# First modulation of a decoder step in two column halves, over the first two tiles of the input projection

## The reference, cut to what matters

```python
def _front(x, c, g_mix, w_ada, b_ada, w_in):
    mod = (jax.nn.silu(c) @ w_ada + b_ada)[:, None, :]
    shift1, scale1, gate1, shift2, scale2, gate2 = jnp.split(mod, 6, axis=-1)
    h = _rmsnorm(x, g_mix) * (1 + scale1) + shift1
    ...
    q, k, v, b_gate, c_gate, u_in, gate_a, gate_b = jnp.split(h @ w_in, pts, axis=-1)
```

## Time and profile before

| | |
|---|---|
| median of 3 runs | 789.85 us (789.43 to 791.33) |
| profiled execution | 789.53 us, span 787.8 us |
| PE busy | 694.5 us, 88% of the span |
| first matmul of tile 0 / of tile 1 | 41.97 us / 50.78 us |
| last `w_ada` of the first modulation landed | 33.37 us |

### The profile page before, as it was taken

The page is one execution under the profiler, slowest core; times in us unless marked ns, Lnnn a source line. Parts: engine busy times, 40 slices in busy tenths (PEclk is TensorE's granted clock), DMA queues, the critical chain, the costliest instruction groups (busy, mean ns, idle before and its releaser), DMA issues.

```text
span 787.8 us, 12170 instructions
## 1 busy us (share of the span) xinstructions
PE 694.5 (88%) x5003; PEld 532.7 (68%) x5003; DVE 318.0 (40%) x701; ACT 165.7 (21%) x323; POOL 123.9 (16%) x189
## 2 busy tenths in 40 slices
PE   2589999999999999999999999779999988788820
PEld 1289989879899889999997455555565554455500
DVE  2162232135688773322234765425232322211235
ACT  4062222221154442112110111111111111100001
POOL 2400000410006001000000100123333332222112
PEclk9989999999999999999999999769999999988975
DMA  9843546856143438421105972779999999999873
GB/s 293 331 160 140 215 174 267 324 215 222 54 133 118 151 105 331 169 69 67 55 27 177 415 294 87 255 291 400 415 414 413 411 413 417 416 414 416 356 302 151
DMA packets 40399, 198.48 MB, mean 252 GB/s; under 512 B 8174, under 2 KB 8358, under 8 KB 24720
## 3 DMA queue, kind: packets, MB, share of 16 engines
q1 hardware_dynamic: 31088, 175.42, 57.3%
q0 software_dynamic: 8352, 21.81, 8.0%
q10 hardware_dynamic: 904, 0.47, 0.3%
HBM read 188.54 MB, written 17.40 MB: 261 GB/s over the span
## 4 chain that ended last, share of the span: by engine, by line
PE 81%; DMA 6%; DVE 4%; issue 4%; ACT 2%; SPq 1%; POOL 1%; POOLq 0%; DVEq 0%
PE bank L1632 31%; PE bank L1878 16%; PE bank L1833 7%; PE bank L1900 7%; DMA arena<-in_w_in 5%; PE bank L1776 4%; PE bank L1871 2%; PE bank L1773 2%; PE bank L1570 2%; PE bank L1668 2%; PE bank L1731 1%; PE bank L1794 1%; PE bank L1895 1%; DMA arena<-y_scratch 1%; PE bank L1714 1%
## 5 line engine op out<-in xcount | busy, mean ns | idle before, releaser
L1632 PE MATMUL bank<-h_parts,w_parts 128*128 128x260 f32 x2160 | 273.4, 286 | 0.8 <-DVE w_parts L1068 0.6
L1632 PEld LDWEIGHTS bank<-h_parts,w_parts 128*128 128x128 f32 x2160 | 263.8, 189 | 9.9 <-issue 8.2
L1878 PE MATMUL bank<-arena,arena_b 128*64 128x256 f32 x704 | 89.8, 412 | 13.5 <-issue 9.1
L1068 DVE TENSOR_TENSOR w_parts<-arena,w_parts 128x1024 fp32r<-128x1024 f32 x46 | 56.2, 1222 | 71.3 <-ACT w_parts L897 71.1
L1878 PEld LDWEIGHTS bank<-arena,arena_b 128*64 128x64 f32 x704 | 57.6, 148 | 39.5 <-issue 12.3
L1422 DVE TENSOR_TENSOR arena_b<-bank,arena_b 128x128 f32<-128x128 f32 x32 | 9.3, 292 | 129.8 <-ACT arena_b L1000 129.7
L897 ACT ACTIVATE w_parts<-arena 128x1024 fp32r<-128x1024 f32 x46 | 48.4, 1052 | 55.9 <-DMA arena<-in_w_in 41.9
L829 POOL DMA_INDIRECT y_scratch<-arena_b x32 | 33.2, 1037 | 161.9 <-DVE arena_b L1447 154.4
L1833 PE MATMUL bank<-arena,arena_b 128*128 128x512 f32 x128 | 56.7, 597 | 0.0
L1878 PE MATMUL bank<-arena_b 128*64 128x256 f32 x320 | 40.1, 407 | 6.1 <-issue 5.3
L1900 PE MATMUL bank<-arena,arena_b 128*64 128x512 f32 x176 | 42.3, 593 | 0.8 <-DVE arena_b L1428 0.8
(11 more groups left out here) (301 smaller groups left out, 761.1 us busy)
## 6 DMA issues: line engine op xcount, KB each, us to landing
arena<-in_w_gate_up SPq DMA_DIRECT2D x44, 1024.0 KB, 29.1
arena<-in_w_in SPq DMA_DIRECT2D x46, 512.0 KB, 4.9
arena<-in_w_ada SPq DMA_DIRECT2D x22, 1024.0 KB, 7.2
arena<-in_w_down SPq DMA_DIRECT2D x20, 1024.0 KB
arena_b<-in_w_gate_up SPq DMA_DIRECT2D x20, 1024.0 KB
arena_b<-in_w_down SPq DMA_DIRECT2D x20, 512.0 KB
arena_b<-in_x_prompt SPq DMA_DIRECT2D x8, 512.0 KB, 7.8
arena_b<-q_scratch POOLq DMA_DIRECT2D x3, 1024.0 KB, 5.7
```

The lines of the kernel that those rows point to most:

```text
L1068: dve.tensor_tensor(w_parts[:, n % 2, 1], ring[:, n % WRING], w_parts[:, n % 2, 0], ALU.subtract).then_inc(s_wlo, 1)
L1632: ins = pe.matmul(ps[s][:, 0:HALF], w_parts[:, n % 2, wp, k], h_parts[:, hp, k, s * HALF:(s + 1) * HALF], start=(k == 0 and hp == 1), stop ...
L1878: ins = pe.matmul(ps[2 + b][R * hh:R * hh + R, 0:2 * P], hTe[:, b, c * P + jj * R:c * P + jj * R + R], w_gu[slot][jj][:, c, :, hh * P:(hh ...
```

## The change

The first modulation is computed in two halves of the features. Half j gives shift1 and scale1 for the 512 features of chunks 4j to 4j + 3. Its weights are laid out ahead in DRAM as `w_ada0`, four DMAs of 1 MB for each half, and each is one `first_step(half, s)`: two chunks by shift and scale, 4 matmuls into four quarters of 32 partitions of one bank, in which even and odd chunks have quarters of their own; a matmul with `both_quarters` (`turn_mods`) turns and adds them. SP issues x, half 0, tiles 0 and 1, half 1. PE does half 0, the chunks 0 to 3 of tile 0, the chunks 0 to 3 of tile 1 (other banks), and then the chunks 4 to 7 of both in turn; the four steps of half 1 stand between those of the chunks 0 to 3. ACT and DVE do `split(1)` within the h of chunks 0 to 3. The bias comes in two lots: ACT issues four DMAs of 9 rows of one piece of 2 KB at the old place, and four of two pieces before chunk 4. DVE's first memset is 2048 columns instead of 1536, and one small addition makes `both_quarters`. Some semaphores are merged. The diff, cut to this:

```diff
-TURNED = (2, 4, 5, 7)
+TURNED = (2, 4, 5, 7, 2, 4, 5, 2)
...
+        ada0 = [[region("SPLIT", (4 + 2 * s) * D, 2 * D) for s in range(4)],
+                [region(("CACHE", "QK")[s // 2], 2 * (s % 2) * D, 2 * D) for s in range(4)]]
+        ada0 = [[r.rearrange("p (k j n) -> p k j n", k=2, j=2) for r in half] for half in ada0]
+        ada = cube(region("CACHE", 0, 4 * D), 2)
...
+        tile_bank = [(ps[3], ps[7]) if n == 1 else (ps[0], ps[1]) for n in range(len(ORDER))]
+        row_bank = [(ps[2 + 2 * (n % 2)], ps[3 + 2 * (n % 2)] if n else ps[6]) for n in range(NQKV)]
+
+        def h_done(k):
+            return k + 2 if k < 4 else k + 3
...
-                if a >= 4:
-                    sp.wait_ge(s_adamm, a)
-                dst = ada0[a] if a < 4 else ada
+                sp.wait_ge(s_adamm, a + 4)
                 for k in range(2):
-                    sp.dma_start(dst[:, k], ada_v[a // 4, a % 4, k]).then_inc(signal, 16)
+                    sp.dma_start(ada[:, k], ada_v[a // 4 - 1, a % 4, k]).then_inc(s_ada[3], 16)
+
+            def load_first(half):
+                for s in range(4):
+                    sp.dma_start(ada0[half][s].rearrange("p k j n -> p (k j n)"), w_ada0[half, s]
+                                 ).then_inc(s_adb[s // 3] if half else s_ada[s], 16)
 
             def load_tile(n):
                 sp.dma_start(ring[:, n % WRING].rearrange("p k n -> p (k n)"), w_in[n]).then_inc(s_win[n % WRING], 16)
 
-            for a in range(4):
-                load_ada(a)
-                if a == 0:
-                    for i in range(5):
-                        sp.dma_start(x[0:rows[i], i], xp_v[i] if i < 4 else xs_v).then_inc(s_x[i], 16)
-            load_tile(0)
-            for n in range(1, len(ORDER)):
+            for i in range(5):
+                sp.dma_start(x[0:rows[i], i], xp_v[i] if i < 4 else xs_v).then_inc(s_x[i], 16)
+            load_first(0)
+            for n in range(WRING):
+                load_tile(n)
+            load_first(1)
+            for n in range(WRING, len(ORDER)):
...
+                sp.wait_ge(s_wlo, n - WRING + 1)
...
+                at = 12 * (j % 2)
+                act.dma_start(ada_bias[32 * j:32 * j + 1 + TS, at:at + 4].rearrange("p s n -> p (s n)"),
+                              b_v[0, j:j + 1].to_broadcast([1 + TS, 512])).then_inc(s_bada, 16)
+                j, cc = k // 4, k % 4
+                if k == 2:
+                    split(1)
+                if k == 4:
+                    for jj in range(4):
+                        act.dma_start(ada_bias[32 * jj:32 * jj + 1 + TS, 4:12].rearrange("p (g s) n -> p g (s n)", g=2),
+                                      b_v[1:3].rearrange("g j n -> j g n")[jj:jj + 1].to_broadcast([1 + TS, 2, 512])
+                                      ).then_inc(s_bada, 16)
+                if cc == 0:
+                    act.wait_ge(s_mod, j + 1)
                 act.wait_ge(s_xT, k + 2)
-                j, cc = k // 4, k % 4
-                at_least(act, s_hD, k - 1)
+                if k >= 3:
+                    act.wait_ge(s_hD, h_done(k - 3))
...
+            def first_out(j):
+
+                if j == 0:
+                    dve.wait_ge(s_bada, 64)
+                dve.wait_ge(s_adamm, 4 * j + 4)
+                dve.tensor_tensor(mods[:, 0:4], cube(ps[6][:], 4), ada_bias[:, 12 * j:12 * j + 4], ALU.add
+                                  ).then_inc(s_adaev, 1)
+                dve.wait_ge(s_modT, j + 1)
+                src = cube((ps[0], ps[6])[j][:, 0:256], 4)
+                shift, scale = 32 * j, 64 + 32 * j
+                dve.tensor_copy(modT[:, :, shift:shift + 1 + TS], src[:, :, 0:1 + TS])
+                link(dve.scalar_tensor_tensor(out=modT[:, :, scale:scale + 1 + TS], in0=src[:, :, 32:33 + TS],
+                                              scalar=1.0, in1=gmixT[:, 4 * j:4 * j + 4].unsqueeze(2)
+                                              .to_broadcast([P, 4, 1 + TS]), op0=ALU.add, op1=ALU.mult))
+                dve.engine_nop().then_inc(s_mod, 1)
+                if j == 0:
+                    split(0)
+
...
+                for k in range(4 * j, 4 * j + 4):
+                    dve.wait_ge(s_hA, k + 1)
+                    if k % 2:
+                        link(dve.tensor_copy(h_parts[:, 0, k, 0:TP], h_tmp[:, k % 3]))
+                    dve.tensor_tensor(h_parts[:, 1, k, 0:TP], h_tmp[:, k % 3], h_parts[:, 0, k, 0:TP], ALU.subtract
+                                      ).then_inc(s_hD, 1)
+                    if k == 2:
+                        split(1)
...
-            for n in range(NQKV):
+            for n in range(1, NQKV):
                 split(n + 1)
-                if n:
-                    by_rows(n - 1)
+                by_rows(n - 1)
...
+            def first_step(half, s):
+
+                if half == 0:
+                    pe.wait_ge(s_ada[s], 16)
+                else:
+                    pe.wait_ge(s_adb[s // 3], 16 if s == 3 else 48)
+                if half and s == 0:
+                    pe.wait_ge(s_adaev, 1)
+                for kk in range(2):
+                    for jj in range(2):
+                        q = 32 * (2 * jj + kk)
+                        ins = pe.matmul(ps[6][q:q + 32, :], cvec[:, 2 * s + kk], ada0[half][s][:, kk, jj],
+                                        start=(s == 0), stop=(s == 3), skip_group_check=True)
+                ins.then_inc(s_adamm, 1)
+
+            def turn_mods(half):
+
+                pe.wait_ge(s_adaev, half + 1)
+                for cc in range(4):
+                    ins = pe.matmul((ps[0], ps[6])[half][:, 64 * cc:64 * cc + 64], mods[:, cc], both_quarters,
+                                    start=True, stop=True, skip_group_check=True)
+                ins.then_inc(s_modT, 1)
+
             def turn_x(k):
-                at_least(pe, s_hA, k - 3)
+                at_least(pe, s_hA, 5 if k == 7 else k - 3)
                 for i in range(NB):
-                    ins = pe.transpose(ps[TURNED[k % 4]][:, i * P:(i + 1) * P], x[:, i, k * P:(k + 1) * P], idn)
+                    ins = pe.transpose(ps[TURNED[k]][:, i * P:(i + 1) * P], x[:, i, k * P:(k + 1) * P], idn)
                 ins.then_inc(s_xT, 1)
 
-            for a in range(2):
-                ada_step(a)
+            def tile_step(n, k):
+
+                if k == 0:
+                    pe.wait_ge(s_whi, n + 1)
+                    pe.wait_ge(s_wlo, n + 1)
+                pe.wait_ge(s_hA, k + 1)
+                pe.wait_ge(s_hD, h_done(k))
+                for s in range(2):
+                    for wp, hp in ((0, 1), (0, 0), (1, 0)):
+                        ins = pe.matmul(tile_bank[n][s][:, 0:HALF], w_parts[:, n, wp, k],
+                                        h_parts[:, hp, k, s * HALF:(s + 1) * HALF],
+                                        start=(k == 0 and hp == 1), stop=(k == KD - 1 and wp == 1),
+                                        skip_group_check=True)
+                    if k == KD - 1:
+                        ins.then_inc(s_half, 1)
+
+            for s in range(4):
+                first_step(0, s)
             pe.wait_ge(s_xn, 5)
             for k in range(KD):
                 ins = pe.transpose(ps[3][:, k * TS:(k + 1) * TS], x[0:TS, 4, k * P:(k + 1) * P], idn[0:TS, 0:TS])
             ins.then_inc(s_xT, 1)
+            turn_x(0)
+            turn_mods(0)
+            for k in range(1, 4):
+                turn_x(k)
+            first_step(1, 0)
+            for k in range(4):
+                if k == 2:
+                    first_step(1, 1)
+                tile_step(0, k)
+                if k < 3:
+                    turn_x(4 + k)
+            first_step(1, 2)
             for k in range(3):
-                turn_x(k)
-            for a in range(2, 4):
-                ada_step(a)
-            turn_x(3)
-            pe.wait_ge(s_adaev, 1)
-            for cc in range(4):
-                ins = pe.transpose(ps[0][:, cc * P:(cc + 1) * P], mods[:, cc], idn)
-            ins.then_inc(s_modT, 1)
+                tile_step(1, k)
+            first_step(1, 3)
+            tile_step(1, 3)
+            turn_mods(1)
+            for k in range(4, KD):
+                if k == 5:
+                    turn_x(7)
+                for n in range(2):
+                    tile_step(n, k)
```

More of the change, by code:

```diff
@@ L1989, in laid_out @@
         out[name] = cached(t[name], s)
-    out |= {name: t[name] for name in ("cache_conv", "c_prompt", "c_sample", "g_mix", "w_ada", "b_ada")}
+    out |= {name: t[name] for name in ("cache_conv", "c_prompt", "c_sample", "g_mix")}
+    first = t["w_ada"][0][:, 0:2 * D].reshape(4, 2, P, 2, 2, 512)
+    out["w_ada0"] = first.transpose(4, 0, 2, 1, 3, 5).reshape(2, 4, P, 2 * D)
+    out["w_ada"] = t["w_ada"][:, :, 2 * D:]
+    out["b_ada"] = t["b_ada"]
     out["w_in"] = w_in[[n for _, n, _ in ORDER]]
```

132 lines of the change are left out of this document (46 added, 86 removed).

## The result

The changed kernel takes 791.85 us (median of 19 runs, 790.36 to 793.06), the kernel before 789.43 us (19 runs, 787.79 to 791.33). The ratio is 1.003, with a 95% interval of 1.0022 to 1.0038: it is slower by about 2.4 us. The forecast was 788.4 us, and the upper end of its range 791.8.

The account below looks back on a forecast made before the run. Loads, then PE's chain, were taken to bound the opening up to tile 2: 55.4 against 57.34 us, gain 1.9, less 0.5 for the clock; 1.4 off 789.53 gives 788.1, median 788.4, range 786.0 to 791.8.

Parts of the forecast that it names:

- What bounds the opening: Up to tile 2's start: loads, then PE's chain; a microsecond saved before tile 2 is kept to the end.
- Term 1: Opening loads: x, half 0, two tiles and three quarters of half 1 landed at 31.0 us, before 33.37.
- T: When three of half 1's four DMAs have landed, letting PE's first projection product start: 31.0 us, bounds 29.9 to 33.0.
- Term 2: PE from T to the second turned modulation: 11.4 us of work plus 2.0 for the low clock, ending at 44.4.
- `turn_mods`, 0.3 us: PE turning the second modulation: four short matmuls, between 0.2 and 0.9 us, taken at 0.3.
- Term 3: PE idle after the second turned modulation until chunk 4 of h is ready: 2.8 us, to 47.2.
- Term 4: Chunks 4 to 7 of both tiles on PE: 6.3 us, PE setting the pace; tile 0 ends at 52.8.
- rival B: Slower: PE loses the clock in the gap before chunk 4, costing 1.7 us; with T at 33.0, 791.6; chance 0.12.
- Term 5: PE waits 1.4 us before tile 2, whose split needs tile 0's buffer; tile 2 starts at 55.4.

Follow-up runs that it names:

- second pair of profiles: The changed kernel and the kernel before, each run unchanged once more for another profile: 792.52 us (4 runs) and 789.5 us (one run).
- second profile: The changed kernel run unchanged once more for another profile: 792.52 us (4 runs), ratio 1.0046 to the kernel before.
- bias_alone: The kernel before with only the modulation's bias in two lots, the second behind the split of tile 2: 786.29 us, ratio 0.9953.
- bias_whole: The changed kernel with all eight bias DMAs issued at the old place: 793.45 us, ratio 1.0045 to the kernel before.
- filler_kept: The changed kernel with 20 spare matmuls behind the second turned modulation, start=False so the output stays right: 788.73 us, ratio 0.9992 to the kernel before.
- filler: The changed kernel with 20 spare matmuls behind the second turned modulation, starting new sums that spoil the output: 788.75 us, ratio 0.9991 to the kernel before.
- gap_covered: The changed kernel with half 1's last step ahead of tile 1 and the turned modulation behind tile 1's chunk 0: 786.83 us, ratio 0.997 to before.
- tile0_first: The changed kernel with chunks 5 to 7 of tile 0 ahead of those of tile 1: 789.78 us, ratio 1.0001 to the kernel before.
- products_ahead: The changed kernel with tile 0's chunks 0 and 1 and two turns of x ahead of half 1's first step: 787.44 us, ratio 0.9982 to before.

## Where the prediction held and where it failed

- *What bounds the opening, and that it carries to the end:* held for the opening; the second half was only half argued. From 64 to 430 us the longest wait of PE is 1.3 us as before, and in the second pair of profiles the lag at tile 2 is nearly that at the end, in the first pair it isn't. The prediction looked for waits up to 430 us only, and took the experts' loads to move along; behind about 630 us PE does wait, with the DMA engines full. In the medians the gains that the traces show at tile 2 came through all the same.
- *The base:* the forecast stood on a median of 789.85 from 3 runs; with 19 it is 789.43. From that base the forecast would have been 788.0 and its miss 3.8 us in place of 3.4.
- *Term 1, T = 31.0:* held (31.01; 30.55 in the second profile, so the 0.01 of the first is luck). The gate on `s_adb0` held the first product back, and the bias moved T; bias_alone and bias_whole show it from both sides. The Trainium skill, page "DMA: Bandwidth & Descriptors", section "Queues, rings and completion order", tells of engines that take turns between queues; with that alone T would have been at 33.0, and the trace disagrees. The prediction priced the second queue's own bytes at 0.5 us; by their share in the earlier trace rows, 13.0% of 8 us, its packets took 1.0, still a third of the 3.1.
- *Term 2, 13.4 us:* the groups and steps were sized nearly right: from T to the turned modulation 13.3 us in the first profile, for 13.1. In the second it was 14.7. Without the low clock the two are 11.6, for 11.1. The low clock after T, taken at 2.0 us, cost 1.65 (31.0 to 34.3 at half speed) and 3.1 (30.55 to 36.8). In the first profile PE reached full speed only while it turned x (from 26.33) and idled 2.65 us before T; in the second it was at full speed from 20.53, so it was done sooner and idled 5.63. The other profiles of this order fit: filler_kept idled 2.38 us and was back at full clock at 34.7; filler, gap_covered and tile0_first idled 4.99 to 5.59 and were back at 35.7 to 36.6. No run varied this idle time by itself, so what sets the length stays open. (In bias_whole PE hadn't reached full speed before T at all; its slow products there are no fall.)
- *`turn_mods`, 0.3 us:* wrong, 1.01 to the next record in the chain (1.11 in the timeline). It was taken as four short records; it is eight (L1619 x8). It lies wholly on the path.
- *Term 3, the gap of 2.8:* held, 2.75 and 2.74.
- *Term 4, and rival B:* this is the step that failed. The chunks 4 to 7 were priced at full speed with 0.5 us off for a fall of the clock, "one chance in three". The clock fell in both profiles of the changed kernel, in tile0_first, bias_whole and products_ahead, that is in all five that kept the gap, and in none of those that filled it. It cost 1.5 us, for 0.5 taken. The argument against B, that dense work ahead of the gap would protect the level, was wrong: from 34.3 to 45.4 us PE was busy at full speed, and it didn't help. The Trainium skill, page "TensorE: Matmul & The Clock Gate", section "HAM oscillation — how this bites in real kernels", tells of a kernel that loses the clock in its waits between bursts. Those waits are longer than this gap, so the page didn't settle the case; the five traces show the loss at 2.75 us. B's own time, 791.6, came out by luck: it took T at 33.0 besides. With T at 31.0 its sum is 55.4 + 1.7 = 57.1 for tile 2, and it was 58.05 and 59.10, by the terms below.
- *Term 5, the new wait:* held, 1.47 for 1.4.

Together: tile 2 was worked out at 55.4, before the 0.5 taken off for the clock. The clock in the gap adds 1.5, the turn 0.7, the rest 0.4 (0.5 in the groups and steps up to the turn and 0.3 behind it, less 0.35 of the low clock after T): 58.05. In the second profile the longer low stretch adds 1.4 and the earlier T takes 0.45: 59.10. The mechanisms were all named; the clock, which has two chances to fall in the new order, was treated as a side issue, and the sign hung on it. At tile 2 the traces have 1.0 to 2.2 us of loss where 1.4 of gain was forecast. The 2.4 that T gains come from the bias, so the halving had in effect been worked out as a loss of 0.5 to 1.0, and it cost 5.5; costing the two apart would have shown where the estimate hung. Of the 5.5 the traces place 3.3 to 4.4 us ahead of tile 2 (58.05 and 59.10 against bias_alone's 54.74); the rest isn't placed.

## What to carry to other kernels

When work is pulled ahead of a transfer, write PE's order so that no hole opens behind it: a hole of 2.75 us cost its length and then 1.5 us of half speed afterwards, and moving work that is ready into it paid both back (5.0 us here, for a few moved lines). Cost a change that carries several edits one by one: here a small DMA in two lots gained 3.3 us and the reordering around it lost 5.5. Two tiles that end together leave no cover for the split of the next; finish the one whose buffer is wanted first. And when a gain is said to carry to the end, look at what sets the pace in every stage up to the end: here the waits of PE were looked at up to 430 us, and the long ones lie behind that.

## What was not expected of the hardware

- With 142 packets (0.22 MB) of a second queue in 8 us the DMA engines brought 260 GB/s in all, 3.1 us lost where these packets' own time is 1.0; with 64 and 72 packets it was 385 and 380, with 165 beside other loads 317.
- The granted clock fell to 0.50 in a gap of 2.75 us or within 1.5 us behind it, in each of the five profiles that kept it, though 9 to 13 us of matmuls at full speed stood before it.
- The granted clock reads 1.00 in bias_whole from 36 to 37 us, and a group of six takes 1.65 us there, 0.97 later. Until 39.5 us PE hadn't once run at full speed in that execution; in this state the column doesn't show that PE is slow, and the duration of a known group does.
- Filling a gap with matmuls whose result nobody reads made the whole kernel 3.1 us faster, 1.5 of them in the stretch behind the gap.
